# Fetching each weight item of a two-layer decoder by two DMAs of half the k-tiles

## Chip, cores and metric

The kernel runs on one core of one Trainium2 chip. The metric is the device time in microseconds of one execution, as the median of several; lower is better.

## What is computed

A small decoder trunk in float32 on 256 tokens of width 2048: one layer of gated linear attention (GLA), then one layer of multi-head latent attention (MLA). Each layer is a mixer and a gated feed-forward part with a causal convolution of width 3, and each is preceded by an RMSNorm whose scale and shift come from a vector `c`.

```python
for i in range(DEPTH):                                   # DEPTH = 2, D = 2048
    mod = c_act @ mod_w[i] + mod_b[i]                    # mod_w: (2, 2048, 12288)
    sh_m, sc_m, g_m, sh_f, sc_f, g_f = jnp.split(mod, 6, axis=-1)
    h = modulate(rmsnorm(x, norm_mix_g[i]), sh_m, sc_m)
    y = gla_mixer(h, ...) if i < N_A_LAYERS else mla_attention(h, ...)
    x = x + (1 + g_m)[:, None, :] * y
    h = modulate(rmsnorm(x, norm_ffn_g[i]), sh_f, sc_f)
    x = x + (1 + g_f)[:, None, :] * conv_ffn(h, ...)     # w_up (2048, 11264), w_down (5632, 2048)
return rmsnorm(x, final_norm_g)
```

All weights are read once from HBM, some 630 MB.

## The kernel before, in words

**Weight items.** Every large product is cut into 378 weight items, numbered in the order in which they are used. A full item is four k-tiles of 128 rows by 512 columns: a tile of 128 partitions by 2048 floats, 1 MB. In the last third of each feed-forward part (`down02`, `down12`) an item has three k-tiles (768 KB), eight items of the MLA query weights are four k-tiles of 384 columns, and two items are narrow (16 k-tiles of 16 or 64 columns). In HBM a row of an item is 2 KB long, so a full item is 512 pieces.

**The ring.** Items pass through a ring of `RAW = 4` slots. SyncE (SP) issues the load of item n in `load_item` (line 449) once TensorE is through with item n - 4 (the semaphore `item_used`). ScalarE (ACT) waits in `hi` for the load (semaphore `raw_in` of the slot, which every DMA raises by 16 when all of it has landed), and rounds the item to `w_hi` (line 649). VectorE (DVE) waits in `lo` for `w_hi` and writes the rest, `w_lo`, in place over `raw` (line 954). TensorE (PE) waits for `w_lo` and runs for each k-tile and each half of the tokens three matmuls (lines 1477 to 1479): `w_hi` with `h_hi`, `w_lo` with `h_hi`, `w_hi` with `h_lo`. A full item is 24 matmuls. ACT and DVE run `hi` and `lo` up to `AHEAD = 3` items ahead, in an order written out by hand between their other work: evacuating PSUM (`u`, line 655 on ACT, 1037 on DVE), splitting activations, and in the feed-forward part the convolution (line 1236), gating and the split of its result (`a_hi` line 808, `a_lo` line 1259).

**The modulation weights.** The 14 vectors of 2048 values that scale and shift the norms are products of one row with 2048 by 2048 matrices. They run on DVE: 224 loads of 1 MB (128 rows, 8 KB each) are multiplied and summed into `acc`. The first 32 (line 464, DVE line 1098) use the two slots of `mods` and the four of `raw` before any weight item is loaded. The other 192 (line 455, DVE line 963) use a ring of two slots `mods`. SP issues them between the items at hand-set places: in some sections with every item, in some with every other item, and in the second layer after `up10` with none. A modulation load waits on SP until DVE is through with the one two before.

**One order on SP.** SP issues everything in program order: where it waits for one thing, all later loads wait too.

```python
for n, src in enumerate(where):
    if n - AHEAD in mod_at:
        load_mod(*mod_at[n - AHEAD])
    ...
    load_item(n, src)
```

The sections come in this order: modulation, `gate`, `qk`, `v`, `r`, `gla_out`, `up00`, `down00`, `up01`, `down01`, `up02`, `down02`, `latent`, `ukv`, `uq`, attention heads, `mla_out`, `up10` to `down12`. `down02` is the one section with 768 KB items that also has a modulation load with each of them.

Of the kernel before, what the change touches and what calls it, by code (L numbers as in the profile page):

```python
# [30 lines left out]
RAW = 4  # L31
# [104 lines left out]
def yoco_kernel(nc, x, c, positions, mod_w, mod_b, norm_mix_g, norm_ffn_g, gla_w_in, gla_w_gate2,  # L136
# [163 lines left out]
    with ExitStack() as ctx:  # L300
        def sem(name):
            return ctx.enter_context(nc.semaphore(name))
# [5 lines left out]
        raw_in = [sem(f"raw_in{i}") for i in range(RAW)]  # L308
# [73 lines left out]
        n = 0  # L382
# [44 lines left out]
        def words_of(n):  # L427

            return NARROW.get(n, ITEM) if isinstance(n, int) else ITEM
# [7 lines left out]
        def _(sp):  # L437
            a = at

            def load_item(n, src):  # L440

                if n < RAW:

                    sp.wait_ge(mod_used, max(m for m in range(FIRST) if m % (MODS + RAW) == MODS + n) + 1)
                else:
                    sp.wait_ge(item_used, n - RAW + 1)
                _, j, width = src.shape
                dst = raw[:, n % RAW, 0:j * width].rearrange("p (j n) -> p j n", j=j)
                sp.dma_start(dst, src).then_inc(raw_in[n % RAW], 16)

            def load_mod(n, g, kt):

# [76 lines left out]
# [3 lines that stand above are left out]
                if n == a["r"].item + 8:  # L532


                    sp.wait_ge(ms_done, made(a["diag"].ms + 1))
                    sp.wait_ge(xq_made, 2 * len(UNITS))
                    sp.dma_start(x_sb[:, :, :], x.rearrange("o (t p) d -> p (o t) d", p=P)).then_inc(x_in, 16)
                load_item(n, src)
                if n == 0:

                    sp.dma_start(wg2[0:RANK, :], gla_w_gate2[0]).then_inc(wg_in, 16)
                    sp.dma_start(wg2[RANK:RANK + 1, :], gla_b_gate).then_inc(wg_in, 16)
# [94 lines left out]
        def _(act):  # L637
# [3 lines left out]
            def hi(n, slot=None):  # L641


                if isinstance(n, int) and n >= TOTAL:
                    return
                k, words = n if slot is None else slot, words_of(n)
                act.wait_ge(raw_in[k % RAW], 16 * ((n - k % RAW) // RAW + 1) if isinstance(n, int)
                            else 4 * (n - k % RAW) + 16)
                act.activation(w_hi[:, k % RAW, 0:words], raw[:, k % RAW, 0:words],  # L649
                               ACT.Copy).then_inc(hi_made, 1)  # L650

# [48 lines left out]
            for n in range(AHEAD + 1):  # L700
                hi(n)
# [12 lines left out]
            for i in range(2):  # L714
                for k in range(8):
                    hi(s.item + AHEAD + 8 * i + k)
                    if i == 0 and k in (1, 2):
                        gate_logs(2 * k - 2)
                        gate_logs(2 * k - 1)
                    if k % 4 == 3:  # L720
                        par = k // 4
                        if par == 0:

                            act.wait_ge(ms_done, made(a["gate"].ms + 8))

                        act.wait_ge(tp_done, s.tp + 4 * i)
                        evac(s.item + 8 * i + k, par, u[:, par])

            s = a["v"]
            for k in range(16):  # L730
                hi(s.item + AHEAD + k)
                w, hh = UNITS[k]
                act.wait_ge(e_made, k + 1)
                act.activation(ex[:, k % 2], ex[:, k % 2], ACT.Exp, scale=1.0 / GATE_NORM).then_inc(f_made, 1)  # L734
                if k % 4 == 3:
                    ch = k // 4
                    evac(s.item + k, ch % 2, v_sb[:, :, ch * W:(ch + 1) * W])
# [157 lines left out]
            for k in range(8):  # L895
# [7 lines left out]
                src = gm[:, k % 2].rearrange("p t (h v n) -> p t h v n", h=2, v=2)  # L903
# [11 lines left out]
            for h in range(MH + 2):  # L915
                if h < MH:
                    act.wait_ge(s_made, h + 1)
                    for b, (c0, c1) in enumerate(((0, 1), (1, 3))):
# [3 lines left out]
                        k = 4 * (h % 2) + b  # L922
# [932 lines left out]
```

## Time and profile before

| what | us |
|---|---|
| median of 3 runs | 2622.3 |
| lowest, highest | 2621.37, 2625.31 |
| span of the profiled execution, first to last instruction | 2625.2 |
| PE busy | 2343.8 (89%) |
| DVE busy | 1883.6 (72%) |
| ACT busy | 1098.7 (42%) |

The profiled execution's span, 2625.2 us, is its own time as far as the profile gives one; it lies within the lowest and highest of the runs, 2.9 us above their median. Spans are divided into stages by the times of the trace, counted from the first instruction. PE is busy for 89% of the span, but which engine sets the pace changes from stage to stage; busy shares over the whole span don't say where a later load would cost time. The chain of work that ended last, and the waits, do.

### The profile page before, as it was taken

To read this page: it belongs to the slowest core of one execution; us is meant where nothing else is said; L and a number is where in the kernel's file an instruction comes from. 1 tells how busy PE (TensorE), PEld (TensorE's weight loads), DVE (VectorE), ACT (ScalarE), POOL (GpSimd) and SP (SyncE) were. 2 spreads that over 40 slices of the span, in tenths; PEclk is the share of its full clock that TensorE was granted. 3 is DMA by queue.
4 is the path that set the end of the run, shared out by engine and by line. 5 is a ranking of instruction groups with operands and counts; after the bars stand their busy time and mean duration, and the time that the engine had idled before them with its cause. 6 is when DMAs were issued, how large, how long until landed. Compare 5 with 4: busy or idle time off the path is not lost.

```text
span 2625.2 us, 26798 instructions
## 1 busy us (share of the span) xinstructions
PE 2343.8 (89%) x10558; PEld 1917.3 (73%) x10558; DVE 1883.6 (72%) x1709; ACT 1098.7 (42%) x1128; POOL 153.5 (6%) x144
## 2 busy tenths in 40 slices
PE   0389989897999999999997798788999999999997
PEld 0267778686887788888875587577788788878875
DVE  6867994676778868786898658768688655655564
ACT  1143342444454345433543533224465445543453
POOL 1030670000000000000000010000000000000000
PEclk9999999998999999999999779889999999999998
DMA  9668776574878978877979259248677455555544
GB/s 357 261 216 329 256 240 236 183 271 163 316 255 298 346 253 295 302 297 259 351 282 357 75 194 326 73 174 306 224 276 284 162 195 188 182 170 193 192 149 155
DMA packets 234040, 632.79 MB, mean 241 GB/s; under 512 B 14385, under 2 KB 19529, under 8 KB 203866
## 3 DMA queue, kind: packets, MB, share of 16 engines
q1 hardware_dynamic: 233370, 627.30, 66.6%
q10 hardware_dynamic: 576, 4.19, 0.4%
q8 instruction: 64, 1.05, 0.2%
q14 instruction: 30, 0.25, 0.0%
HBM read 629.36 MB, written 2.10 MB: 241 GB/s over the span
## 4 chain that ended last, share of the span: by engine, by line
PE 68%; DVE 15%; DMA 6%; issue 5%; ACT 4%; SPq 0%; POOL 0%; DVEq 0%; POOLq 0%; ACTq 0%
PE gm L1477 21%; PE gm L1479 21%; PE gm L1478 21%; DVE acc L1098 3%; DMA raw<-in_ffn_w_down_dram 3%; DVE acc L963 3%; PE tp L1493 2%; DVE w_lo L954 2%; ACT w_hi L649 2%; PE ms L1529 2%; DVE conv L1236 1%; DMA raw<-in_ffn_w_up_dram 1%; DVE both L1012 1%; DMA raw<-in_gla_w_in_dram 1%; DVE h_lo L1016 1%
## 5 line engine op out<-in xcount | busy, mean ns | idle before, releaser
L954 DVE TENSOR_TENSOR w_lo<-raw,w_hi 128x2048 fp32r<-128x2048 f32 (+2 forms) x378 | 856.9, 2271 | 443.6 <-ACT w_hi L649 442.4
L649 ACT ACTIVATE w_hi<-raw 128x2048 fp32r<-128x2048 f32 (+2 forms) x378 | 702.9, 1863 | 789.4 <-DMA raw<-in_ffn_w_up_dram 241.6
L1477 PE MATMUL gm<-w_hi,h_hi 128*128 128x512 f32 x1952 | 774.9, 397 | 3.5 <-DVE w_lo L954 3.5
L1479 PE MATMUL gm<-w_hi,h_lo 128*128 128x512 f32 x1952 | 765.4, 392 | 0.0
L1478 PE MATMUL gm<-w_lo,h_hi 128*128 128x512 f32 x1952 | 765.1, 392 | 0.0
L963 DVE SCALAR_TENSOR_TENSOR acc<-mods,c_col,acc 128x2048 f32<-128x2048 f32 x192 | 450.3, 2346 | 2.6 <-DMA mods<-in_mod_w_dram 2.6
L1477 PEld LDWEIGHTS gm<-w_hi,h_hi 128*128 128x128 f32 x1952 | 370.3, 190 | 81.1 <-issue 6.9
L1479 PEld LDWEIGHTS gm<-w_hi,h_lo 128*128 128x128 f32 x1952 | 369.4, 189 | 78.8
L1478 PEld LDWEIGHTS gm<-w_lo,h_hi 128*128 128x128 f32 x1952 | 369.9, 190 | 74.5
L1477 PE MATMUL gm<-w_hi,a_hi 128*128 128x512 f32 x736 | 298.7, 406 | 19.3 <-DVE a_lo L1259 10.1
L1478 PE MATMUL gm<-w_lo,a_hi 128*128 128x512 f32 x736 | 292.9, 398 | 0.0
L1479 PE MATMUL gm<-w_hi,a_lo 128*128 128x512 f32 x736 | 292.8, 398 | 0.0
L1236 DVE SCALAR_TENSOR_TENSOR conv<-tp,cv_col,conv 128x255 f32<-128x255 f32 (+1 forms) x352 | 152.6, 477 | 103.6 <-ACT conv L795 95.2
L1477 PEld LDWEIGHTS gm<-w_hi,a_hi 128*128 128x128 f32 x736 | 142.4, 193 | 56.5 <-DVE a_lo L1259 13.3
L655 ACT ACTIVATE u<-gm 128x1024 f32<-128x1024 f32 (+1 forms) x90 | 90.1, 1001 | 195.0 <-PE gm L1479 187.1
L1478 PEld LDWEIGHTS gm<-w_lo,a_hi 128*128 128x128 f32 x736 | 142.3, 193 | 30.8 <-issue 1.4
L1479 PEld LDWEIGHTS gm<-w_hi,a_lo 128*128 128x128 f32 x736 | 141.8, 193 | 30.6
L795 ACT ACTIVATE conv<-tp,cv_col 128x256 f32<-128x256 f32 x176 | 88.3, 560 | 117.1 <-PE tp L1493 116.9
L1529 PE MATMUL ms<-ones,acc 128*128 128x1 f32 x320 | 51.1, 294 | 88.7 <-DVE acc L1098 73.6
L1529 PEld LDWEIGHTS ms<-ones,acc 128*128 128x128 f32 x320 | 51.2, 253 | 90.9 <-DVE acc L1098 74.0
L1493 PE MATMUL tp<-ident,u 128*128 128x128 f32 x464 | 73.5, 287 | 31.3 <-DVE conv L1236 14.0
L613 POOL TENSOR_TENSOR ex<-ex,qk_t 128x512 f32<-128x512 f32 x32 | 88.9, 2795 | 147.6 <-ACT ex L734 147.6
(198 smaller groups left out, 1704.9 us busy)
## 6 DMA issues: line engine op xcount, KB each, us to landing
raw<-in_ffn_w_up_dram SPq DMA_DIRECT2D x176, 1024.0 KB, 5.1
mods<-in_mod_w_dram SPq DMA_DIRECT2D x172, 1024.0 KB, 7.1
raw<-in_ffn_w_down_dram SPq DMA_DIRECT2D x64, 1024.0 KB, 5.1
raw<-in_gla_w_in_dram SPq DMA_DIRECT2D x48, 1024.0 KB, 5.3
mods<-in_kv_mod_w_dram SPq DMA_DIRECT2D x32, 1024.0 KB, 7.1
raw<-in_ffn_w_down_dram SPq DMA_DIRECT2D x32, 768.0 KB, 5.5
raw<-in_mod_w_dram SPq DMA_DIRECT2D x20, 1024.0 KB, 7.5
raw<-in_gla_w_o_dram SPq DMA_DIRECT2D x16, 1024.0 KB, 5.0
```

The lines of the kernel that those rows point to most:

```text
L613: pool.tensor_tensor(f, f, s, ALU.mult).then_inc(xq_made, 1)
L649: act.activation(w_hi[:, k % RAW, 0:words], raw[:, k % RAW, 0:words], ACT.Copy).then_inc(hi_made, 1)
L655: act.activation(dst, gm[:, par] if src is None else src, func).then_inc(u_made, 1)
L795: ins = act.activation(conv[:, j % 2, side, :], tp[:, bank, side * T:(side + 1) * T], ACT.Identity, scale=cv_col[:, layer, 2, cs], bias=cv ...
L954: dve.tensor_tensor(w_lo[:, k % RAW, 0:words], raw[:, k % RAW, 0:words], w_hi[:, k % RAW, 0:words].bitcast(F32), ALU.subtract).then_inc(lo ...
L963: dve.scalar_tensor_tensor(acc[:, g % 2, :], mods[:, slot, :], ck, acc[:, g % 2, :], ALU.mult, ALU.add).then_inc(mod_used, 1)
L1236: ins = dve.scalar_tensor_tensor(v, tp[:, bank, side * T:(side + 1) * T - shift], cv_col[:, layer, tap, cs], v, ALU.mult, ALU.add)
L1477: pe.matmul(o, hi_s[:, kt, tok], wh[:, j, :], start=kt == 0, stop=False)
L1478: pe.matmul(o, hi_s[:, kt, tok], wl[:, j, :], start=False, stop=False)
L1479: ins = pe.matmul(o, lo_s[:, kt, tok], wh[:, j, :], start=False, stop=kt == total - 1)
L1493: ins = pe.transpose(tp[0:m, bank, col:col + k], src, ident[0:k, 0:k])
L1529: ins = pe.matmul(o[:, j:j + 1], acc[:, g % 2, j * P:(j + 1) * P], ones[:, 0:1], start=True, stop=True)
```

## The change

`load_item` issues two DMAs in place of one. The first fetches the first `j // 2` k-tiles of the item, the second the others; both go out of SP one behind the other, with no wait between them, and both raise the same semaphore by 16. The wait in `hi` is for 32 for each use of the slot in place of 16, so ACT still starts on an item only when all of it has landed. An item of three k-tiles is fetched as one and two. Modulation loads, all other loads, the ring and the order are as they were.

```diff
                 _, j, width = src.shape
                 dst = raw[:, n % RAW, 0:j * width].rearrange("p (j n) -> p j n", j=j)
-                sp.dma_start(dst, src).then_inc(raw_in[n % RAW], 16)
+                sp.dma_start(dst[:, 0:j // 2, :], src[:, 0:j // 2, :]).then_inc(raw_in[n % RAW], 16)
+                sp.dma_start(dst[:, j // 2:j, :], src[:, j // 2:j, :]).then_inc(raw_in[n % RAW], 16)
...
-                act.wait_ge(raw_in[k % RAW], 16 * ((n - k % RAW) // RAW + 1) if isinstance(n, int)
-                            else 4 * (n - k % RAW) + 16)
+                act.wait_ge(raw_in[k % RAW], 32 * ((n - k % RAW) // RAW + 1) if isinstance(n, int)
+                            else 8 * (n - k % RAW) + 32)
                 act.activation(w_hi[:, k % RAW, 0:words], raw[:, k % RAW, 0:words],
                                ACT.Copy).then_inc(hi_made, 1)
```

## Rows read from the trace of the kernel before

**Rows 1.** The page: busy share of PE in 40 slices of the span, in tenths.

```profile
PE   0389989897999999999997798788999999999997
```

**Rows 2.** The whole span, waits: us in total, times, longest.

```profile
DVE w_lo L954 <- ACT w_hi L649: 442.4, 191, 11.9
...
ACT w_hi L649 <- DMA raw<-in_ffn_w_up_dram: 241.6, 77, 5.5
...
PE gm L1477 <- DVE w_lo L954: 12.4, 9, 2.0
...
DVE acc L963 <- DMA mods<-in_mod_w_dram: 2.6, 3, 1.4
```

**Rows 3.** Windows: us; PE, PEld, DVE, ACT, POOL busy; clock, DMA share, GB/s.

```profile
2109.00:2285.00 176.00, 176.00 (x800) 145.63 (x800) 100.72 (x100) 83.93 (x84) 0.00 (x0) 1.00 0.56 186
```

**Rows 4.** Timelines of one item in that stretch (start us, us, engine).

```profile
2147.09 0.37 SPq L449 DMA_DIRECT2D raw<-in_ffn_w_up_dram  x1
2151.98 1.92 ACT L649 ACTIVATE w_hi<-raw 128x2048 fp32r<-128x2048 f32 x1 [2.38 <-DMA raw<-in_ffn_w_up_dram]
2153.93 2.29 DVE L954 TENSOR_TENSOR w_lo<-raw,w_hi 128x2048 fp32r<-128x2048 f32 x1 [2.92 <-ACT w_hi L649]
2163.22 0.39 PE L1477 MATMUL gm<-w_hi,h_hi 128*128 128x512 f32 x1
```

**Rows 5.** The chain that ended last: four of its 20 item loads (start us, us).

```profile
144.55 5.06 DMA raw<-in_gla_w_in_dram
...
596.41 9.48 DMA raw<-in_ffn_w_up_dram
...
1344.03 9.18 DMA raw<-in_ffn_w_down_dram
...
2533.98 4.44 DMA raw<-in_ffn_w_down_dram
```

**Rows 6.** The chain in `down02`, start us and us.

```profile
1391.11 0.34 SPq L455
...
1391.50 8.67 DMA raw<-in_ffn_w_down_dram
```

**Rows 7.** Windows, a stretch of `down02`, columns as in rows 3.

```profile
1387.00:1412.00 25.00, 21.22 (x89) 16.23 (x89) 22.38 (x14) 8.37 (x6) 0.00 (x0) 1.00 0.91 334
```

**Rows 8.** Line 449, 2109 to 2517 us: 72 loads of 1 MB.

```profile
L449 SPq DMA_DIRECT2D raw<-in_ffn_w_up_dram x56: 367/368/368, 2109.0 to 2511.7; - x56
...
DMA to landing us min/median/max: 4.9/5.0/5.6
```

**Rows 9.** Timeline of SP in `down02`, an item's issue.

```profile
1387.57 0.43 SPq L449 DMA_DIRECT2D raw<-in_ffn_w_down_dram  x1
```

**Rows 10.** Timeline and line 449 of items 1 and 2, issued back to back.

```profile
97.89 0.39 SPq L449 DMA_DIRECT2D raw<-in_gla_w_in_dram  x1
...
98.33 0.51 SPq L449 DMA_DIRECT2D raw<-in_gla_w_in_dram  x1
...
DMA to landing us min/median/max: 5.2/5.2/5.2
...
DMA to landing us min/median/max: 7.5/7.5/7.5
```

**Rows 11.** Line 449, 2517 to 2595 us: 16 loads of 768 KB.

```profile
DMA to landing us min/median/max: 4.1/4.3/4.4
```

**Rows 12.** DMA view, 2109 to 2114.2 us, one load of 1 MB alone, 40 slices of 0.13 us.

```profile
GB/s 0 0 0 0 0 0 0 0 173 126 79 47 79 95 126 173 362 362 378 378 441 394 378 457 410 378 425 394 425 410 378 457 394 268 79 0 0 0 0 0
DMA packets 528, 1.05 MB, mean 202 GB/s; under 512 B 16, under 2 KB 16, under 8 KB 528
```

**Rows 13.** DMA view, 97.8 to 106.8 us, the same two loads and a third, slices of 0.225 us.

```profile
GB/s 9 206 91 0 18 100 100 91 127 255 364 346 391 410 382 437 419 410 391 391 419 428 400 400 400 410 428 364 382 419 382 364 410 364 391 400 355 410 400 346
```

**Rows 14.** Timelines of SP: two issues right behind an item's.

```profile
863.45 0.50 SPq L455 DMA_DIRECT2D mods<-in_kv_mod_w_dram  x1
...
585.95 1.50 SPq L455 DMA_DIRECT2D mods<-in_mod_w_dram  x1
```

## Prediction

> **What bounds the kernel now.** I read the page first. PE is busy for 89% of the span, and its slices are at nine tenths through most of it [rows 1]. In the matmul stages PE sets the pace. Next come the waits: ACT waits long for item loads and DVE waits 442.4 us for ACT, but PE waits only 12.4 us, nine times, for a `w_lo` that isn't there [rows 2]. So most of the waiting for loads lies on engines that are ahead of PE, where it costs nothing. The stretch from 2109 to 2285 us shows it: PE is busy for all 176 us, with the DMA engines at 0.56 [rows 3]. One item of it, step by step: issued at 2147.09, `w_hi` starts at 2151.98, `w_lo` starts at 2153.93 and ends 2.29 us later at 2156.22, and PE begins the item at 2163.22 [rows 4]. That item could land 7.0 us later and PE would not notice.
>
> Where does the landing of an item matter, then? The chain that ended last passes through 20 item loads, the first at 144.55 us and the last at 2533.98 [rows 5]. They are of two kinds. Six are loads that moved almost alone and took 4.4 to 5.1 us each, as the first and the last of them: there ACT stands in its fixed order at `hi`, and behind that stands convolution or splitting work that PE needs soon. The other 14 took longer, up to the 9.48 us at 596.41, because a modulation load was under way too. Five of these lie close together in and just behind `down02`, the first at 1344.03, and there a load of 768 KB takes 8.67 us [rows 6] while the DMA engines are busy for 0.91 of the stretch at 334 GB/s [rows 7]: those wait for bandwidth, not for an issue. So the question is by how much, call it d, an item lands later (or earlier) when it comes in halves, and the first estimate is 20 times d.
>
> **The change, part by part.**
>
> One DMA goes, two come: 378 more issues on SP. An issue takes 0.37 us [rows 8]; the one right behind it may take 0.43 to 0.51. That is 378 x 0.37 = 140 us more on SP in all, up to 193 with 0.51. It is hidden, because SP mostly waits. From 2109.0 to 2511.7 it issued 72 items [rows 8], one every 402.7 / 71 = 5.7 us, so it has some 4.8 us to spare each time. In `down02` an item's issue ended at 1387.57 + 0.43 = 1388.00 [rows 9], and the next issue began at 1391.11 [rows 6], 3.1 us later; one more issue of 0.5 us fits. Cover gone, it would cost 0.4 to 0.5 us for each load behind it.
>
> The second half is issued some 0.42 us after the first (0.37 and the 0.05 us that lie between two issues: 98.33 - 97.89 - 0.39 [rows 10]). Is it then late? A 1 MB load alone takes a median of 5.0 us [rows 8], one of 768 KB 4.3 us [rows 11]; a quarter of an item is 0.7 us. By that line a half alone would land after 3.6 us, and the second half alone after 0.42 + 3.6 = 4.0 us, before the 5.0 of the whole. So the issue isn't what ends the load; the data is. The trace of one load says the same: nothing moves for 8 slices of 0.13 us after the issue, about 1.0 us more go at 47 to 173 GB/s, and then some 400 GB/s flow to the end [rows 12]. The second half's order is out 0.6 us before the first byte of the first half moves. d from the issue: 0.
>
> What could lie between the halves is a pause at the boundary of two DMAs. Rows that show one are those of items 1 and 2, issued 0.44 us apart. They landed at 97.9 + 5.2 = 103.1 and 98.3 + 7.5 = 105.8 us [rows 10]: 2.7 us apart, and 4 x 0.7 = 2.8 us is what four quarters of pure data take. In between the flow never falls below 346 GB/s once it is up, with no dip where one load ends and the other begins [rows 13]. So the pause is 0, between -0.1 and +0.1 us. The first of the two landed after 5.2 us in place of 5.0, with small loads just ahead of it; I keep +0.2 as the upper end of d.
>
> The Trainium skill ("SBUF — State Buffer", The DMA setup-cost knee; "DMA: Bandwidth & Descriptors", Rules for kernel authors) speaks against this change: every transfer pays a roughly fixed 2 us, and loads should be 1 MB or more. By that rule, if the second half paid its 2 us on the path, the sum would be 20 x 2 = 40 us. The pair in the trace disagrees as far as throughput goes: 2.7 us for the second MB leaves no room for it.
>
> More signals: each DMA ends with 16 small packets, 528 = 512 + 16 [rows 12]. With 378 more DMAs that is 6048 more packets. Even if each took as long as a piece of 2 KB, one for each of 16 engines per load would be 1/32 of the 2.7 us that a load's data takes, 0.08 us; they carry 4 bytes, so I take 0.01 to 0.08 us, and 0.05 with whatever else a boundary has.
>
> The modulation load that follows an item at once goes out 0.45 us later, and its issue may stall: 0.50 us is usual, 1.50 us the worst seen [rows 14]. DVE waited only 2.6 us in the whole span for such a load [rows 2], so they have their slack. If the stall came back at every tenth load it would still lie in SP's spare time. The higher threshold on ACT costs nothing: the same wait, the same queue behind it (`w_hi`, then what ACT has for PSUM and the convolution), and it is as late as the load is, which is counted in d.
>
> Sum: 20 x 0.05 = +1.0 us, with ends 20 x -0.1 = -2 and 20 x 0.2 = +4 us. The span of 2625.2 becomes 2626.2; it stands 2.9 us above the median of the runs, so for the runs 2622.3 + 1.0 = 2623.3, own range 2620.3 to 2626.3.
>
> **The rivals.**
>
> A. A pause after all (slower). The halves are two DMAs in the same queue. The signal of the first might hold up the writes of the second for 0.3 to 0.9 us in a load that moves alone, where the pair above, which began behind small loads, doesn't speak for it. Price: 20 x 0.3 to 0.9 = +6 to +18 us, so 2628 to 2640. It decides from d = 0.26 us on, where 20 d passes 5.2 us, which is 0.2% and about what a measurement of this kernel can tell from no change. Against it: [rows 13]. For it: no row, only that no row shows two loads in a row out of a quiet state. Chance 0.10.
>
> B. The halves run one after the other in full, the second starting when the first has landed: 3.6 + 3.6 = 7.2 us in place of 5.0, 20 x 2.2 = +44 us, 2666. [rows 10] contradict it. Chance 0.02. The fixed 2 us of the Trainium skill (same pages and sections) would give nearly this, 2622 + 40 = 2662.
>
> C. Faster. In [rows 12] the flow is at 47 to 173 GB/s for its first microsecond. If that is the time in which a large order is being broken into its pieces, a smaller first order would be up sooner, perhaps by a third of it, 0.3 us: 20 x -0.3 = -6 us, 2616. Against it: two loads in a row show the slow start once, and the load of 768 KB gains on 1 MB only what its bytes are worth. ACT doesn't start before both halves are in, so a part that lands early is of no use by itself. Chance 0.06. The Trainium skill ("Perfetto Trace Analysis", DMA Optimizations) says that splitting may end the whole sooner where the DMA engines are mostly idle; in the quiet stretch they are idle for 0.44 of the time [rows 3], and no run here shows yet whether it helps.
>
> D. SP becomes late. In stages with modulation loads, a second issue behind a full queue may stall for 1.5 us, and the modulation load behind it waits too; DVE then waits at `acc` and holds up `w_lo`. In `down02` 16 items x 0.5 us = +8 us, 2630. It needs stalls that use up the 3.1 us of spare time. Chance 0.03.
>
> **How the numbers follow.** No measurable change, 0.79, at 2623.3; A 0.10, B 0.02, C 0.06, D 0.03. Faster by over 0.2% is C and a little of the tail, 0.07; slower is A, B and D less what of A and D stays small, 0.14; the rest, 0.79, is within 0.2%. The range has to hold 8 in 10: the forecast's own range, with a run's scatter of about 3 us either way, has 0.79; I take it down to 2617 and up into the lower part of A and D, 2630.
>
> **What would show it.** Right: 756 issues at line 449; 6048 more packets; the second half lands within 5.2 us of the first half's issue in the stretch of [rows 8]; PE busy for all of [rows 3]'s stretch; the `down02` loads of [rows 6] at 8 to 9 us from the first half's issue; PE's wait for `w_lo` near 12 us. Wrong: landings of 5.3 us or more from the first issue in the quiet stretch (A), of 7 (B), of 4.7 or less (C); issues above 1 us on SP and DVE waiting for `mods` by more than 10 us (D). A change of the order in which the pieces of an item are read from HBM could alter the flow of 400 GB/s itself; no row tells of that, and it would show in the quiet stretch too.

## The result, and the profile after

| | median us | lowest to highest |
|---|---|---|
| before | 2621.37 | 2616.88 to 2625.31 (5 runs) |
| after | 2631.71 | 2628.58 to 2634.8 (5 runs) |

The ratio is 1.0043, with a 95% interval of 1.0029 to 1.0058: the change makes the kernel 10 us slower, where no measurable change (2623.3, range 2617 to 2630) was forecast.

Four parts of the page of the kernel after, whose lines stand one further down in the code than before (the DMA line; the groups of `w_hi` and of `acc`; the DMA issues of section 6, with KB each and the median us to landing):

```profile
span 2631.8 us, 27176 instructions
...
DMA packets 240091, 632.84 MB, mean 240 GB/s; under 512 B 20433, under 2 KB 25577, under 8 KB 209914
...
L650 ACT ACTIVATE w_hi<-raw 128x2048 fp32r<-128x2048 f32 (+2 forms) x378 | 703.2, 1863 | 816.9 <-DMA raw<-in_ffn_w_up_dram 241.6
...
L964 DVE SCALAR_TENSOR_TENSOR acc<-mods,c_col,acc 128x2048 f32<-128x2048 f32 x192 | 450.2, 2345 | 4.3 <-DMA mods<-in_mod_w_dram 4.1
...
raw<-in_ffn_w_up_dram SPq DMA_DIRECT2D x352, 512.0 KB, 4.6
mods<-in_mod_w_dram SPq DMA_DIRECT2D x172, 1024.0 KB, 6.9
raw<-in_ffn_w_down_dram SPq DMA_DIRECT2D x160, 512.0 KB, 4.8
```

The change did what it says: twice the issues, of half the bytes. The one sum that grew is ACT's idle time before `w_hi`: 816.9 us. The same group of the kernel before reads:

```profile
L649 ACT ACTIVATE w_hi<-raw 128x2048 fp32r<-128x2048 f32 (+2 forms) x378 | 702.9, 1863 | 789.4 <-DMA raw<-in_ffn_w_up_dram 241.6
```

So ACT waits 27.5 us more for items. DVE's wait for modulation loads is 4.1 us after and was 2.6 [rows 2], and PE's for `w_lo` is next to unchanged (waits of the kernel after: total, times, longest):

```profile
PE gm L1478 <- DVE w_lo L955: 13.4, 10, 2.0
```

PE's late starts are spread over many small waits further down ACT's and DVE's fixed orders, and no single wait of PE shows them. Their sum does: the span less PE's busy time, both on the page, is 2625.2 - 2343.8 = 281.4 us before and 2631.8 - 2345.3 = 286.5 us after.

In the quiet stretch nothing changed. Windows of the kernel after, columns as in [rows 3], over the same work:

```profile
2114.00:2290.00 176.00, 176.00 (x800) 145.66 (x800) 100.72 (x100) 84.20 (x84) 0.00 (x0) 1.00 0.57 186
```

PE is busy for all of it, as in [rows 3]. Line 450, the second half, from 2114 to 2517 us, and SP's timeline of one item there:

```profile
L450 SPq DMA_DIRECT2D raw<-in_ffn_w_up_dram x55: 368/471/943, 2114.4 to 2512.9; - x55
...
DMA to landing us min/median/max: 4.5/4.7/5.2
```

```profile
2114.02 0.37 SPq L449 DMA_DIRECT2D raw<-in_ffn_w_up_dram  x1
2114.43 0.47 SPq L450 DMA_DIRECT2D raw<-in_ffn_w_up_dram  x1
```

The second half is out 0.41 us after the first and lands 4.7 us later, so 5.1 us after the item's first issue, where a whole item took 5.0 [rows 8]. There d is 0.1 us, as forecast.

In the stages with modulation loads it is otherwise. Timeline of SP in `qk`, then lines 449 and 450 from 170 to 240 us of the kernel after:

```profile
188.99 0.37 SPq L449 DMA_DIRECT2D raw<-in_gla_w_in_dram  x1
189.41 0.47 SPq L450 DMA_DIRECT2D raw<-in_gla_w_in_dram  x1
189.92 0.47 SPq L456 DMA_DIRECT2D mods<-in_mod_w_dram  x1
```

```profile
DMA to landing us min/median/max: 3.9/5.4/6.0
...
DMA to landing us min/median/max: 4.9/7.2/7.9
```

The second half lands 0.42 + 7.2 = 7.6 us after the first issue. The same window of the kernel before, line 449, whole items:

```profile
L449 SPq DMA_DIRECT2D raw<-in_gla_w_in_dram x11: 367/368/368, 170.6 to 236.8; - x11
...
DMA to landing us min/median/max: 5.0/6.1/6.7
```

That is 1.5 us more by the medians of this window. Over all 16 items of `qk` the means, worked out from each item's first issue and last landing, are 5.96 us before and 6.96 after, so d is 1.0 there. The chain that ended last, of the kernel after, still passes through 19 item loads, four of them in `down02` (start us of the part's own issue, us):

```profile
1347.67 10.53 DMA raw<-in_ffn_w_down_dram
1376.49 8.40 DMA raw<-in_ffn_w_down_dram
1397.65 8.74 DMA raw<-in_ffn_w_down_dram
1419.16 8.63 DMA raw<-in_ffn_w_down_dram
```

The third is a second half, issued 0.48 us behind its first (SP's timeline of the kernel after):

```profile
1397.17 0.43 SPq L449 DMA_DIRECT2D raw<-in_ffn_w_down_dram  x1
1397.65 0.53 SPq L450 DMA_DIRECT2D raw<-in_ffn_w_down_dram  x1
```

Counted from there it took 9.22 us, against 8.67 in [rows 6].

The first load of the chain, the item at 144.55 in [rows 5], took 5.06 us from issue to landing, and the prediction put it among the six that "moved almost alone". SP's timeline of the kernel before has a modulation load right behind it; then, of the kernel after, the same item and its line of the chain:

```profile
144.55 0.37 SPq L449 DMA_DIRECT2D raw<-in_gla_w_in_dram  x1
144.96 0.50 SPq L455 DMA_DIRECT2D mods<-in_mod_w_dram  x1
```

```profile
145.02 0.37 SPq L449 DMA_DIRECT2D raw<-in_gla_w_in_dram  x1
145.43 0.47 SPq L450 DMA_DIRECT2D raw<-in_gla_w_in_dram  x1
...
145.43 6.05 DMA raw<-in_gla_w_in_dram
```

In halves it landed 0.41 + 6.05 = 6.46 us after its first issue, 1.4 us more than whole. The other profiles of whole items and of halves say the same: 5.22 us in whole_again, 6.44 and 6.33 in halves_again and busy_only. But the item took 6.53 us in tiny_behind too, a kernel told of below that keeps it whole and loses nothing that can be told. So the load was not alone, and its landing moved by much more than 0.1 us; that this one lateness costs time is not shown.

### The profile page after: what moved, and what is told of

Same layout as the page of the kernel before. It is cut to its first block, busy times and chain, and to the rows that moved or that the text cites. A ratio compares the mean times of both kernels' runs of the same rounds, so it can differ in the third digit from the quotient of the medians.

```text
span 2631.8 us, 27176 instructions
## 1 busy us (share of the span) xinstructions
PE 2345.3 (89%) x10558; PEld 1917.7 (73%) x10558; DVE 1883.9 (72%) x1709; ACT 1098.7 (42%) x1128; POOL 150.8 (6%) x144
## 2 busy tenths in 40 slices
DMA packets 240091, 632.84 MB, mean 240 GB/s; under 512 B 20433, under 2 KB 25577, under 8 KB 209914
## 4 chain that ended last, share of the span: by engine, by line
PE 68%; DVE 15%; DMA 6%; issue 5%; ACT 4%; SPq 1%; POOL 0%; DVEq 0%; POOLq 0%; ACTq 0%
PE gm L1478 21%; PE gm L1479 21%; PE gm L1480 21%; DVE acc L1099 3%; DMA raw<-in_ffn_w_down_dram 3%; DVE acc L964 3%; PE tp L1494 2%; DVE w_lo L955 2%; PE ms L1530 1%; DVE conv L1237 1%; ACT w_hi L650 1%; DVE both L1013 1%; DMA raw<-in_gla_w_in_dram 1%; DVE h_lo L1017 1%; DVE ex L1180 1%
## 5 line engine op out<-in xcount | busy, mean ns | idle before, releaser
L650 ACT ACTIVATE w_hi<-raw 128x2048 fp32r<-128x2048 f32 (+2 forms) x378 | 703.2, 1863 | 816.9 <-DMA raw<-in_ffn_w_up_dram 241.6
```

## The experiments

Two theories to begin with. **Division**: data that comes in more DMAs flows worse where the DMA engines are saturated. **Lateness**: the last byte's DMA is issued some 0.4 us later (0.41 us in the median, 0.48 in `down02`), and where loads are close to the path that costs time, however the data is cut. The rivals of the prediction (a pause, a late SP) were in play too. Runs marked with the same letter were timed on one chip beside the same runs of the kernel before (medians: a 2621.46, b 2617.57, c 2620.62, d 2620.23).

| run | what it does | median us | ratio [95%] |
|---|---|---|---|
| tiny_behind (a) | whole item, a small DMA behind it | 2623.99 | 1.0006 [0.9995, 1.0017] |
| tiny_before (a) | a small DMA, then the whole item | 2625.51 | 1.0017 [1.0002, 1.0032] |
| busy_only (a) | halves up to `up10`, whole from `down10` | 2635.17 | 1.0047 [1.0031, 1.0063] |
| four_parts (a) | four parts (three where narrower) | 2642.03 | 1.0074 [1.0058, 1.0091] |
| partition_halves (b) | 64 + 64 partitions | 3043.63 | 1.1613 [1.1588, 1.1638] |
| quiet_only (b) | halves from `down10` on alone | 2625.74 | 1.0028 [1.0013, 1.0044] |
| down02_only (b) | halves for the 16 items loaded during `down02` alone | 2621.5 | 1.0016 [1.0003, 1.0029] |
| item_first (b) | whole; item ahead of modulation load | 2637.86 | 1.0077 [1.0058, 1.0097] |
| whole_again (c) | whole items, control | 2622.47 | 1.0007 [0.999, 1.0023] |
| quiet_again (c) | as quiet_only | 2618.24 | 0.9999 [0.9987, 1.0011] |
| halves_again (c) | as the kernel after | 2633.62 | 1.0049 [1.0031, 1.0067] |
| three_one (c) | three k-tiles, then one | 2625.99 | 1.0027 [1.0015, 1.0039] |
| tiny_before_again (d) | as tiny_before | 2627.55 | 1.0029 [1.0015, 1.0044] |
| two_before (d) | two small DMAs, then the whole item | 2651.89 | 1.0111 [1.0093, 1.0128] |
| mods_halved (d) | whole items, modulation loads in halves | 2619.97 | 0.9999 [0.9986, 1.0011] |

One caution holds for all of it: kernels of one kind scatter. Spans of profiled executions with whole items lay between 2608.7 us (down02_only, with 16 halved items) and 2631.6 (whole_again), so a few microseconds between two single profiles are no reading. What is said below rests on medians of several runs or on what repeats in all kernels of a kind.

Most of the scatter lies in PE's busy time and goes with the granted TensorE clock: PE was busy for 2334.8 us at a mean clock of 0.960 in the first of these two profiles and for 2352.2 us at 0.951 in the second. In the 90 timed runs of the kernel before, too, the slower ones had the lower clock (correlation -0.65 to -0.81 on each chip). The span less PE's busy time is steadier, and it sorts the kernels:

| profiled kernels | span less PE's busy time, us |
|---|---|
| before, whole_again, quiet_only, quiet_again, tiny_behind, mods_halved, down02_only | 273.9 to 281.4 |
| after, halves_again, busy_only | 285.9 to 286.5 |
| tiny_before, tiny_before_again | 285.3, 279.1 |
| three_one; four_parts; two_before | 283.0; 293.0; 300.1 |

**Where: busy or quiet.** The number of parts is a function of the item, and the wait in `hi` counts the parts of all earlier uses of the slot:

```diff
-                sp.dma_start(dst, src).then_inc(raw_in[n % RAW], 16)
+                cuts = [j * i // parts_of(n) for i in range(parts_of(n) + 1)]
+                for lo_, hi_ in zip(cuts, cuts[1:]):
+                    sp.dma_start(dst[:, lo_:hi_, :], src[:, lo_:hi_, :]).then_inc(raw_in[n % RAW], 16)
...
+            # busy_only: 2 if n < at["down10"].item + AHEAD else 1; quiet_only and quiet_again: the opposite
+            # down02_only: 2 for the 16 items loaded during down02; whole_again: 1; halves_again: 2
```

> Halves only for the 277 items up to the third of the second layer's first down part, whose neighbours include all modulation loads; the last 101 items are one DMA each. All three theories put the cost where modulation loads are under way: +9 to +11 us. My prediction's way of counting (20 late loads, three of them among the last 101, all late by the same) would leave 17/20 of the loss, +9 us; so this run and its complement are read by the landing times of the two parts too.

> Halves only for the last 101 items, where no modulation load is under way. Both theories, and my prediction: 3 late loads on the chain x 0.1 us = +0.3 us, no measurable change (-2 to +3). If it is +2 us or more, a quiet stage pays too.

> Halves only for 16 items, those loaded during the third down part of the first layer (13 of its items and 3 behind), the one stage in which the chain runs through several item loads while modulation loads fill the DMA engines. In one profile of the change this stage took 5.3 us more than before. Theory 'saturated stage': +4 to +6 us from these 16 items alone. If the cost is spread evenly over the 276 items with busy neighbours: 16/276 x 12 = +0.7 us.

Then, to tell scatter from effect:

> A control: one DMA per item, the instructions of the kernel before. Every theory says ratio 1.000. It shows what a comparison of equal kernels gives here, since halves for the quiet items alone came out 0.28% slower although no stage with those items took longer in the profile. If the control is at 1.001 to 1.002, such differences are the comparison's and not the change's.

> The same kernel as the one with halves for the last 101 items only, a second time. If the quiet stages cost nothing (what the stages in the profiles say): within 0.1% of the control. If they do cost something: +0.2 to +0.3% again.

> The change itself again, on the same chip and against the same runs as the control and the quiet halves: +0.4% again, and a second profile of it. Stages that took longer in the first profile by more than the scatter (qk, r, down00, down02) should again; the up stages not.

busy_only has the whole cost (1.0047, beside 1.0043 and 1.0049 of the full change). quiet_only gave 1.0028 and its repeat 0.9999; the two intervals don't meet, and the stage times decide (here and below each is counted from the first matmul of one section to that of the next): `up11` takes 179.9 us in every kernel with whole items or halves. In the quiet stages halves cost nothing. down02_only, at 1.0016, is too close to the scatter to read; in its one profile `down02` took 119.6 us, as with whole items, and not the 4 to 6 us more that the theory of a saturated stage expected. A first reading, that `down02` alone (118.9 us before, 5.3 longer after) held half of the cost, fell with the control: over the kernels the means of the stage times with halves (the kernel after, halves_again, busy_only) less those with whole items (before, whole_again, quiet_only, quiet_again, tiny_behind and, but for `down02`, down02_only) are +2.0 us in `qk`, +2.1 in `r`, +1.9 in `down00` and +4.3 in `down02`, 10 us in all. Each of the four has modulation loads, but so do ten others, each of which moved by less than 1 us. Only in `down02` do the two groups lie apart (118.2 to 120.6 us with whole items, 122.5 to 124.2 with halves); in the other three the difference is of the size of the scatter, and their shares are not shown one by one.

**Lateness or signals: small DMAs.** A DMA of one value per partition, on semaphores and a tile of its own, behind or ahead of each item's load:

```diff
+                if n >= RAW:
+                    sp.wait_ge(spare_in[n % RAW], 16 * (n // RAW))
+                sp.dma_start(spare[:, n % RAW, 0:1], src[:, 0, 0:1],
+                             allow_slow_non_contiguous=True).then_inc(spare_in[n % RAW], 16)
                 sp.dma_start(dst, src).then_inc(raw_in[n % RAW], 16)
```

> Each item by one whole DMA as before, and right behind it a DMA of one float per partition of the same item into a spare tile, on a semaphore for which only SP waits, four items later. Theory 'count' (each more DMA in SP's queue costs the loads around it): slower by 8 to 12 us, like the change. Theory 'lateness' (the second half is issued 0.47 us after the first and lands that much later where other loads are under way): 0 to 2 us, since the item itself is issued as early as before. Theory 'division' (the data itself flows slower when an item's pieces come in two groups): 0 us.

> As the run with the small DMA behind, but the small DMA goes out of SP ahead of the whole item, which is issued 0.42 to 0.47 us later. Count: +8 to +12 us. Lateness: +6 to +12 us, and landings counted from the small DMA's issue 0.4 us longer than before. Division: 0 us.

Behind the item it costs nothing that can be told (1.0006, interval to 1.0017): neither the 378 further issues nor their signals are the cause, nor that the modulation load behind goes out later by one small DMA's issue. Ahead of the item it costs 4 us, with an interval from 0.5 to 8.

**How it is cut.** Four parts, one of three k-tiles and one of one, and partitions in place of k-tiles:

```diff
+            # four_parts: parts_of(n) = 4 if words_of(n) != UP_BLOCKS[2] * W else 3
+                cuts = [0, j - max(1, j // 4), j]                    # three_one
...
+                sp.dma_start(dst[0:P // 2], src[0:P // 2]).then_inc(raw_in[n % RAW], 16)      # partition_halves
+                sp.dma_start(dst[P // 2:P], src[P // 2:P]).then_inc(raw_in[n % RAW], 16)
```

> Each item by four DMAs of one k-tile (three where it has three). Lateness: the last part is issued 3 x 0.47 = 1.4 us after the first; if landings follow it, +30 us, and quiet landings near 5.3 us from the first issue. Count: three times the loss, +25 to +35 us. Division: near +10 again or up to twice that. If queue room on SP is the matter: issues well above 0.5 us and DVE waiting for modulation loads.

> Two DMAs per item, three k-tiles and then one. The last part is issued 0.47 us after the first but is a quarter of the data, so it can't be late by its issue: 3 k-tiles alone need 4.3 us. Lateness of the second issue as the cause: 0 to +0.1%. Each further DMA with data costing flow in saturated stages as the cause: +0.4% as with halves, and the flow in milliseconds with busy DMA engines near that of the change (394 GB/s against 402).

> Two DMAs per item as in the change, but the first brings all k-tiles for partitions 0 to 63 and the second for 64 to 127. So the number of DMAs, signals and bytes is that of the change, and the pieces of one partition stay together in one DMA, as before. Known so far: a small extra DMA ahead of each item costs +4 us though items land as late as with the change, so 6 of the change's 10 us come with the division of the data. If the order in which rows are read is what slows the flow (k-tiles 0 and 1 of all partitions, then 2 and 3), this run is at +4 us. If any division into two DMAs of full weight costs it, +10 us. If a DMA over 64 partitions is worse by itself, quiet landings grow beyond 5.5 us and the time by more than +10.

Four parts cost 19 us (the last quarter is issued 1.3 us after the first, in the median), three and one 5 to 7. That is more than the 0 to 0.1% that lateness of the issue expected of three and one: beside modulation loads its items still landed later than whole ones, by 0.2 us in the mean. partition_halves is another matter, told at the end.

**The order with the modulation load.**

```diff
-                if n - AHEAD in mod_at:
-                    load_mod(*mod_at[n - AHEAD])
...
                 load_item(n, src)
+                if n - AHEAD in mod_at:
+                    load_mod(*mod_at[n - AHEAD])
```

> Whole items as before, but SP issues each item's load ahead of the modulation load that stood before it. If late landings of items in mixed stages are what costs time, items that don't queue behind a modulation load of 1 MB land up to 2.7 us sooner there, and the kernel gains 5 us or more; if SP then holds modulation loads back behind waits for a free item slot, DVE waits for them and it loses. I expect the gain and the loss to be visible in the two kinds of wait, and the sum between -15 and +20 us.

The items did land sooner (`down02` 6.7 us in the mean, 8.1 before), and ACT's idle time before `w_hi` fell; but DVE now waits for `mods`, in its own order ahead of `w_lo`, and the kernel is 0.8% slower. From the page (ACT) and the waits of item_first:

```profile
L649 ACT ACTIVATE w_hi<-raw 128x2048 fp32r<-128x2048 f32 (+2 forms) x378 | 702.9, 1863 | 725.5 <-DMA raw<-in_ffn_w_up_dram 215.3
```

```profile
DVE acc L963 <- DMA mods<-in_mod_w_dram: 155.6, 89, 11.2
DVE acc L963 <- DMA mods<-in_kv_mod_w_dram: 33.8, 22, 8.8
```

**Lateness against division.** tiny_before left from none to nearly all of the cost to lateness. So the lateness was doubled (two small DMAs ahead of the item, 0.85 us), and the number of DMAs in the saturated stretches was raised with hardly any lateness of the items:

```diff
+                for c in (0, D // 2):                                # mods_halved; and its wait counts by 32
+                    sp.dma_start(mods[:, n % MODS, c:c + D // 2], w[kt * P:kt * P + P, col + c:col + c + D // 2])\
+                        .then_inc(mod_in[n % MODS], 16)
```

> A repeat, to make its interval narrower: one DMA of one value per partition goes out of SP ahead of every whole item, so that each item's load is issued some 0.45 us later, and its data is still one DMA. 'Late' (the cost of the halves is that the second half is issued 0.48 us after the first): most of the halves' cost, ratio 1.003 to 1.005. 'Count' (the cost is that the data itself comes in two DMAs where the engines are saturated): 1.000 to 1.002. First measurement: 1.0017 [1.0002, 1.0032].

> Two such small DMAs ahead of every item, which is issued some 0.9 us later and still comes as one DMA. 'Late': twice the cost of one, so 1.006 to 1.010, of the size of four parts (whose last quarter is issued 1.4 us after the first). 'Count': twice what one costs, 1.002 to 1.004, clearly under the halves. In the quiet stages PE has 7 us of cover, so nothing there in either.

> Items are whole; each of the 192 modulation loads behind the first 32 comes as two DMAs of half the columns (rows of 4 KB in place of 8 KB). Only the stages that have modulation loads are touched. 'Count': more full DMAs and more packets in just the stretches where the halves cost 10 us: 1.002 to 1.005. 'Late': the modulation loads have slack of their own on DVE (2.6 us of waiting in the whole span), so only an item that follows one at once, as in down02, is issued 0.45 us later: 1.000 to 1.002. If it is 1.000, the number of full DMAs in a saturated stretch isn't the cost in itself.

mods_halved is at 0.9999, and its items land as before (`down02`, line 449 from 1338 to 1425 us of mods_halved; 8.5 was the median in the kernel before):

```profile
DMA to landing us min/median/max: 6.4/8.2/9.1
```

So more DMAs full of data in just those stretches are not a cost in themselves, though they do lower the flow: in the slices of 1 us in which the DMA engines were over 95% busy it averaged (worked out from all DMA records of each trace, each counted where it starts) 402.4 GB/s before, 393.7 after and 394.3 in mods_halved. So division, as a loss of flow, is not the cause. Lateness holds: two_before costs 29 us with whole items. SP's timelines show by how much the item's load is put off: 0.42 us in `down02` of tiny_before_again (0.37 in the median of all items), and 0.85 us from the first small DMA in two_before:

```profile
1394.89 0.38 SPq L453 DMA_DIRECT2D spare<-in_ffn_w_down_dram  x1
1395.31 0.43 SPq L455 DMA_DIRECT2D raw<-in_ffn_w_down_dram  x1
```

```profile
1396.22 0.80 SPq L454 DMA_DIRECT2D spare<-in_ffn_w_down_dram  x2
1397.07 0.43 SPq L456 DMA_DIRECT2D raw<-in_ffn_w_down_dram  x1
```

One could object that a small DMA's own packets hold the item up as well. They add little: over the 220 items whose load overlapped a modulation load in the kernel before, an item landed later, counted from the first DMA of its slot, by 0.48 and 0.52 us in the mean with one small DMA and by 1.12 us with two. That is 0.1 to 0.3 us more than the later issue alone.

In `down02` a later whole item can bring nearly the loss that halves bring. Windows of that stage, columns as in [rows 3], for before, after, tiny_before, tiny_before_again and two_before, in this order:

```profile
1343.45:1462.32 118.87, 81.74 (x354) 64.49 (x352) 99.36 (x85) 49.46 (x55) 2.69 (x3) 0.86 0.73 272
```

```profile
1345.91:1470.10 124.19, 82.69 (x354) 65.48 (x352) 100.04 (x85) 49.92 (x56) 2.69 (x3) 0.83 0.71 263
```

```profile
1341.17:1463.88 122.71, 82.33 (x353) 65.01 (x352) 100.30 (x85) 50.82 (x56) 2.70 (x3) 0.85 0.72 264
```

```profile
1337.72:1457.07 119.35, 83.21 (x353) 65.58 (x352) 98.58 (x84) 49.43 (x55) 2.69 (x3) 0.84 0.73 269
```

```profile
1355.91:1481.91 126.00, 83.06 (x354) 65.47 (x352) 100.06 (x85) 50.43 (x56) 2.69 (x3) 0.84 0.72 259
```

PE's idle time in the stage (its length less PE's busy time) is 37.1, 41.5, 40.4, 36.1 and 42.9 us. It comes in two sizes: 36.1 to 37.4 us in all seven kernels of the table's first row, in three_one and in tiny_before_again, and 40.4 to 42.9 us in the three with halves, in four_parts, in two_before and in tiny_before. So the loss of some 4 us there is a step that lateness of a whole item can set off, in one profile of two at 0.4 us of it; what decides on which side of the step a run falls was not looked into.

ACT's idle time before `w_hi` follows the lateness too. The same group of the page in whole_again, mods_halved, tiny_before_again, four_parts and two_before, in this order:

```profile
L657 ACT ACTIVATE w_hi<-raw 128x2048 fp32r<-128x2048 f32 (+2 forms) x378 | 702.8, 1863 | 787.4 <-DMA raw<-in_ffn_w_up_dram 232.2
```

```profile
L650 ACT ACTIVATE w_hi<-raw 128x2048 fp32r<-128x2048 f32 (+2 forms) x378 | 702.8, 1863 | 793.4 <-DMA raw<-in_ffn_w_up_dram 237.4
```

```profile
L655 ACT ACTIVATE w_hi<-raw 128x2048 fp32r<-128x2048 f32 (+2 forms) x378 | 703.3, 1864 | 818.0 <-DMA raw<-in_ffn_w_up_dram 247.4
```

```profile
L657 ACT ACTIVATE w_hi<-raw 128x2048 fp32r<-128x2048 f32 (+2 forms) x378 | 703.6, 1864 | 875.2 <-DMA raw<-in_ffn_w_up_dram 272.0
```

```profile
L656 ACT ACTIVATE w_hi<-raw 128x2048 fp32r<-128x2048 f32 (+2 forms) x378 | 703.5, 1864 | 894.7 <-DMA raw<-in_ffn_w_up_dram 284.8
```

Idle time and kernel time rise together in the main: 776 to 793 us in the kernels that cost nothing or next to nothing, 800 in three_one (+0.3%), 811 to 817 for the halves (+0.45%), 814 and 818 for tiny_before and its repeat (+0.2 and 0.3%), 875 (+0.7%), 895 (+1.1%). The small DMA ahead of the item brings as much of this idle time as the halves, for half of their cost by the medians.

## Why the prediction was wrong

**Right.** What bounds the kernel; the count of issues and of packets (240091 - 234040 = 6051, forecast 6048); the issue of 0.37 and 0.47 us; SP's spare time; no pause between halves, and d of 0.1 us in the quiet stretch; the loads of 768 KB at 8 to 9 us (8.74 in the mean, though the one at 1397 took 9.22). The modulation loads kept their slack: DVE's wait rose by 1.5 us, not by 10, so rival D is out. Rivals A, B and C are out too: 5.1 us in the quiet stretch, where A needed 5.3, B 7 and C 4.7.

**The step that failed** is "d from the issue: 0", with the sentence that the loads beside a modulation load "wait for bandwidth, not for an issue". The value of 0 was read from a load that moved alone, where the second half's order is out before the first byte flows, and it was carried to all 20 loads of the chain. In 14 of them a modulation load was under way, and in three of the other six, at 144.55, 268.84 and 1607.01, one was issued 0.4 to 0.5 us behind the item, so only three moved alone. The runs showed that the time of the issue counts: putting off a whole item by about 0.4 us cost 4.5 and 7.6 us (2621.46 x 0.0017, 2620.23 x 0.0029), and by 0.85 us 29 us (2620.23 x 0.0111), while the number of DMAs (mods_halved, tiny_behind) cost nothing that can be told. Measured from the first issue, d is 1.0 us in `qk`, 0.8 in `gla_out`, 0.6 in `down02` (8.11 to 8.74 in the mean), 0.3 in the median and 0.5 in the mean over the 220 items whose load overlapped a modulation load, and 0.1 in the quiet stages. The prediction's d of 0.05 had no part for this.

**The sum redone.** 6 x 0.1 + 14 x 0.3 to 1.0 = 5 to 15 us, with the 10 measured in the middle of it, where 14 loads cost 0.7 each. The load at 144.55, counted with 0.1, landed 1.4 us later. The form of the sum gives the right size, though no run shows that each load of the chain adds its own d, and its d for the mixed loads was mis-sized: 0.05, with an upper end of 0.2, where 0.3 to 1.0 stands. The time fell into the price of rival A, 2628 to 2640, but not by A's mechanism, a pause in a load that moves alone. The bound itself had been in reach: the prediction named 0.4 to 0.5 us a load as the price if cover were gone, and 14 x 0.45 = 6 us would have moved the forecast to 2629.

**Where the scale of d was missed.** Neither the Trainium skill ("SBUF — State Buffer", The DMA setup-cost knee) with its fixed 2 us per transfer nor a cost of nothing fits: the halves' 10 us over 20 loads is 0.5 us each. The 40 us that the prediction worked out from it is four times what was measured.

**What stays open.** Lateness of a whole item by as much as the second half's explains 4.5 to 7.6 of the 10 to 13 us that halves cost in three measurements (ratios 1.0043, 1.0047 and 1.0049). The rest, some 5 us, may go with the way the item is cut, which is not shown: the intervals of halves (from 1.0029) and of the small DMA ahead (to 1.0044) overlap, and in `down02` one profile with the small DMA has nearly the whole loss. Three and one (1.0027, interval to 1.0039) lies lower than halves, though the intervals of the two overlap too. Lateness of the issue alone does not account for the load at 144.55 either: from its own issue it took 5.1 and 5.5 us in the two profiles with the small DMA ahead, but 6.5 in halves and in tiny_behind, where a second DMA stands between the item's first and the modulation load. Why it lands later there was not isolated. Nor was it found why double the lateness costs four to six times as much.

No version was clearly faster than the kernel before: whole items of 1 MB with the modulation load in its place was the best order tried.

## What to carry to other kernels

Read the price of one more issue ahead of a load's last byte where the load is contended, not where it moves alone: a wait that ends after a shared queue can still be moved one for one by the issue, or by more. When a ring's consumer waits for all parts of an item, each part behind the first only puts off the last byte. Before a stage difference of a few microseconds in two single profiles is believed, profile a control that is the old kernel again; here it alone moved the span by 6.4 us (2625.2 to 2631.6). PE's idle time, which leaves out what the granted clock does to PE's busy time, moved by 2.0 us between the same two profiles (281.4 to 279.4), and by 5.1 us with the change.

## What was not expected of the hardware

**Partitions in place of k-tiles.** Here a DMA of 64 partitions moved at about half the rate of one of 128: at some 200 to 280 GB/s through most of an item's load in the quiet stretch, where [rows 12] has some 400. The DMA view of partition_halves, 2602.9 to 2612 us, slices of 0.23 us:

```profile
GB/s 135 99 36 9 0 0 54 144 72 207 351 387 306 234 216 207 225 198 234 279 243 234 198 225 198 207 117 54 18 0 0 0 108 126 81 135 261 360 387 261
```

Line 450, from 2450 to 2850 us of partition_halves, the second 64 partitions of 1 MB items:

```profile
DMA to landing us min/median/max: 6.2/6.7/8.1
```

With the 0.6 us of the first issue that is 7.3 us in the quiet stretch, against 5.0 for a whole item [rows 8]. In `qk` the same items took 13.9 us in the mean, the slices with busy engines carried 255 GB/s in place of 402, and the waits of partition_halves show PE short of items:

```profile
PE gm L1478 <- DVE w_lo L955: 184.3, 90, 6.0
```

The Trainium skill ("SBUF — State Buffer", Door 1: The DMA port swizzle) says that the rate depends on how many of the 16 ports a transfer's partitions reach, and that 64 partitions in a row reach half of them. The trace agrees in direction: with both halves of an item issued one behind the other, the flow was 255 of 402 GB/s, 0.63 of it and not quite as low as half.

**Flow without effect.** Cutting data into more DMAs took 2% off the flow of saturated slices (402.4 to 393.7 and 394.3 GB/s), and in mods_halved the kernel's time didn't follow: its modulation loads had slack. **Lateness that grows.** One small DMA ahead of each item cost 4.5 to 7.6 us, two cost 29.
